# One transformer step: 30 weight pieces are issued from GpSimd's queue in place of SyncE's

## The reference, cut to what matters

```python
mod = silu(cond) @ w_ada + b_ada          # w_ada: 2048 x 12288 f32, for c (latents) and c_ctx (prompt)
sh1, sc1, g1, sh2, sc2, g2 = split(mod, 6)
h = rms_norm(x, norm1_g) * (1 + sc1) + sh1
z = h @ w_in                              # q, k, v of two attentions, and gate logits
o_g, o_d = gqa_attention(...), diff_attention(...)
merged = gate_a * (o_g @ w_branch_a) + gate_b * (o_d @ w_branch_b)
x = x + g1 * (merged @ w_out)
h2 = rms_norm(x, norm2_g) * (1 + sc2) + sh2
x = x + g2 * peer_layer(h2, peer_w_query, ...)   # 128 gathered experts per token
y = rms_norm(x, final_norm_g)
```

## Time and profile before

| | |
|---|---|
| median of 3 runs | 5230.48 us (5229.95 to 5242.82) |
| the profiled execution | 5234.13 us, of it 5232.3 us span |
| TensorE busy in the span | 3333.8 us (64%) |
| VectorE busy | 2689.3 us (51%) |
| GpSimd busy | 1815.6 us (35%) |
| bytes moved | 1885.12 MB, 360 GB/s over the span |
| q0 (GpSimd's DMAs) | 1347.98 MB |
| q1 (SP's DMAs) | 535.33 MB |

### The profile page before, as it was taken

One profiled execution on the slowest core, in us unless ns is written; L12 is line 12 of the kernel. 1 busy time (PEld: TensorE's weight loads), 2 busy tenths in 40 slices (PEclk: granted clock), 3 DMA queues, 4 the chain that ended last, 5 costly groups with the idle time before them and its releaser, 6 DMA issues.

```text
span 5232.3 us, 32559 instructions
## 1 busy us (share of the span) xinstructions
PE 3333.8 (64%) x11312; PEld 1263.2 (24%) x11312; DVE 2689.3 (51%) x3921; ACT 414.4 (8%) x785; POOL 1815.6 (35%) x1365
## 2 busy tenths in 40 slices
PE   4869888898788898899986390001333333333566
PEld 1333343343344443444442240000000000000000
DVE  2320119897133201576758757998655656565200
ACT  0010000000222110111010010000000000000000
POOL 0000003354322000344435334667445454454333
PEclk7979999999799999999998695555555555555566
DMA  9979976898998687898989878889999999999998
GB/s 379 375 272 352 368 256 264 332 367 345 386 365 321 236 294 271 338 379 352 382 343 388 334 316 340 340 350 397 418 421 418 418 418 418 421 418 418 418 415 367
DMA packets 412273, 1885.12 MB, mean 360 GB/s; under 512 B 30544, under 2 KB 34160, under 8 KB 241760
## 3 DMA queue, kind: packets, MB, share of 16 engines
q0 software_dynamic: 187200, 1347.98, 63.5%
q1 hardware_dynamic: 224928, 535.33, 27.6%
HBM read 1845.08 MB, written 39.42 MB: 360 GB/s over the span
## 4 chain that ended last, share of the span: by engine, by line
DMA 43%; PE 36%; DVE 13%; issue 3%; POOL 2%; ACT 1%; SPq 0%; DVEq 0%; POOLq 0%; ACTq 0%; PEldq 0%
PE ps L795 29%; DMA activations<-in_peer_v,zt 27%; DVE big L1859 5%; DMA big<-in_peer_v,zone 4%; DMA big<-in_peer_u,sel 3%; DMA big<-in_w_in 2%; DMA big<-in_w_ada 2%; PE ps L1133 2%; DMA big<-in_peer_v,sel 2%; DVE big L1605 1%; PE ps L895 1%; POOL big L778 1%; DMA big<-in_w_out 1%; PE ps L955 1%; PE ps L846 1%
## 5 line engine op out<-in xcount | busy, mean ns | idle before, releaser
L795 PE MATMUL ps<-big,activations 128*128 128x512 f32 x4096 | 1797.4, 599 | 115.8 <-ACT zt L1144 38.0
L1859 DVE CUSTOM_DVE_ANT_0 big<-big,activations 128x2048 f32<-128x2048 f32 x384 | 867.3, 2290 | 503.2 <-DMA big<-in_peer_u,sel 479.6
L795 PEld LDWEIGHTS ps<-big,activations 128*128 128x128 f32 x4096 | 778.3, 192 | 1122.8 <-issue 1020.2
L778 POOL DMA_INDIRECT big<-in_peer_u,sel x384 | 565.8, 1473 | 581.9 <-DVE zt L1859 497.4
L1133 PE MATMUL ps<-activations 128*32 128x512 f32 x1536 | 352.2, 1009 | 458.1 <-DMA activations<-in_peer_v,zt 458.1
L1133 PE MATMUL ps<-big,activations 128*32 128x512 f32 x1536 | 353.2, 1014 | 431.1 <-DMA big<-in_peer_v,zt 428.3
L1540 DVE CUSTOM_DVE_ANT_0 big<-big 128x2048 f32<-128x2048 f32 x128 | 291.6, 2292 | 146.1 <-DMA big<-in_peer_u,sel 105.6
L1550 DVE SCALAR_TENSOR_TENSOR big<-big,work 128x2048 f32<-128x2048 f32 x128 | 301.0, 2352 | 90.0 <-DMA big<-in_peer_v,sel 87.5
L753 POOL DMA_INDIRECT big<-in_peer_u,sel x128 | 225.9, 1765 | 316.0 <-DVE zone L1605 279.0
L735 POOL DMA_INDIRECT big<-in_peer_v,sel x128 | 235.0, 1836 | 280.9 <-DVE big L1550 219.8
L735 POOL DMA_INDIRECT big<-in_peer_u,sel x128 | 202.5, 1582 | 328.4 <-DVE work L1540 264.4
(11 more groups left out here) (189 smaller groups left out, 2444.5 us busy)
## 6 DMA issues: line engine op xcount, KB each, us to landing
big<-in_w_in SPq DMA_DIRECT2D x84, 2048.0 KB, 9.3
big<-in_w_ada SPq DMA_DIRECT2D x48, 2048.0 KB, 12.4
big<-in_w_out SPq DMA_DIRECT2D x24, 2048.0 KB, 13.0
big<-in_peer_w_query SPq DMA_DIRECT2D x24, 2048.0 KB, 8.8
big<-in_w_branch_a SPq DMA_DIRECT2D x12, 2048.0 KB, 23.3
big<-in_w_branch_b SPq DMA_DIRECT2D x12, 2048.0 KB, 8.8
big<-z_blocks SPq DMA_DIRECT2D x20, 512.0 KB, 14.5
big<-in_peer_u,sel POOLq DMA_INDIRECT x640
```

The source lines that it names most:

```text
L778: pool.indirect_dma_start(u_slot(m), None, eu, bass.IndirectOffsetOnAxis(ap=sel[:, t % 2, k:k + 1], axis=0)).then_inc(u_in[m % UR], 16)
L795: ins = nc.tensor.matmul(bank(bk), acts[:, k, b * P:(b + 1) * P], w[:, n % WS, k], start=(start and k == 0), stop=(stop and k == KT // 2 - 1))
L1859: V.tensor_tensor_reduce(out=x, in0=x, in1=h_of[ph], scale=1.0, scalar=0.0, op0=ALU.mult, op1=ALU.add, accum_out=dots_b[ph % 2][:, st * TO ...
```

## The change

The 30 pieces from 18 on are no longer issued by SP but by GpSimd, in its loop over the panels. Before it waits for panel p, GpSimd issues pieces 4p+1 to 4p+4. Their landings count on three semaphores of their own, `late_in`, one for each slot; what TensorE waits for is recounted (`late_before` gives how many of these pieces went to the slot before). The waits for `w_free`, the order of TensorE's work, the slots and the bytes are the same.

```diff
+LATE = sorted(RING_AT["ada", i] for i in range(ADA_FIRST, 4 * ADA_PR))
+def late_before(n):
+    return sum(m < n and m % WS == n % WS for m in LATE)
...
+        late_in = [sem(f"late_ada_loaded{i}") for i in range(WS)]
...
                 for c in range(QKV_CH):
-                    if p == 0:
-                        ada(A_QKV + c)
                     if c + 1 < QKV_CH:
                         for j in range(2):
                             half(...)
-                    elif p == 0:
-                        ada(A_ATT)
-                        ada(A_ATT + 1)
...
                     keys(0)
                     sp.dma_start(skn..., sub).then_inc(sk_in, 16)
-                    for i in range(2, 5):
-                        ada(A_ATT + i)
...
-                if g == 0:
-                    ada(A_ATT + 5)
...
                     for c in range(DCH):
-                        ada(A_BR + 2 * c)
                         for j in range(2, 6):
                             half(RING_AT["br", 6 * c + j], 0, 0, br(c, j))
-                        ada(A_BR + 2 * c + 1)
...
-                    if g == 0:
-                        ada(A_OUT + c)
...
-                    if g == 0 and c < DCH - 1:
-                        ada(A_QRY + c)
...
+            def ada(i):
+                n = RING_AT["ada", i]
+                pool.wait_ge(w_free, n + 1)
+                pool.dma_start(w_wide[:, n % WS], w_ada[...]).then_inc(late_in[n % WS], 16)
+
             for p in range(ADA_PR):
+                for i in range(4 * p + 1, 4 * p + 5):
+                    if ADA_FIRST <= i < 4 * ADA_PR:
+                        ada(i)
                 pool.wait_ge(ada_sum, p + 1)
                 pool.dma_start(mod[:, p * ADA_W:(p + 1) * ADA_W], ada_st[p % 2]).then_inc(ada_out[p % 2], 16)
                 pool.wait_ge(ada_out[p % 2], 16 * (p // 2 + 1))
                 if p + 2 < ADA_PR:
                     bias(p + 2)
...
             def wait_half(n, i, step):
-                pe.wait_ge(w_in_sem[n % WS], 16 * (n // WS + 1) + i * (16 * step // WS))
+                if n in LATE:
+                    pe.wait_ge(late_in[n % WS], 16 * (late_before(n) + 1))
+                else:
+                    pe.wait_ge(w_in_sem[n % WS], 16 * (n // WS + 1 - late_before(n)) + i * (16 * step // WS))
```

More of the change, by code:

```diff
@@ L713, in _ @@
                                         pattern=[[-1, P]], channel_multiplier=1).then_inc(mats, 1)
+            def ada(i):
+                n = RING_AT["ada", i]
+                pool.wait_ge(w_free, n + 1)
+                pool.dma_start(w_wide[:, n % WS], w_ada[:, (i % 4) * 4:(i % 4) * 4 + 4, (i // 4) * ADA_W:(i // 4 + 1) * ADA_W]).then_inc(late_in[n % WS], 16)
             for p in range(ADA_PR):
+                for i in range(4 * p + 1, 4 * p + 5):
+                    if ADA_FIRST <= i < 4 * ADA_PR:
+                        ada(i)
                 pool.wait_ge(ada_sum, p + 1)
```

## The result

The changed kernel takes 5259.4 us in median of 6 runs (5253.23 to 5263.1), the kernel before 5230.22 (5226.53 to 5242.82). The ratio is 1.0052, with an interval of 1.0038 to 1.0066: 29 us slower. The profiled execution has a span of 5260.7 us, 28.4 above the one before.

What follows compares the result with a forecast made beforehand. TensorE and the DMA engines were taken as both within 5% of full, so arrival order decides. Terms of +8 (qkv), +2.5 (attention), +9 (br) and +9 (out and qry) gave +28.5 us: 5259 in median, range 5228 to 5276.

Steps and rivals of the forecast that it cites:

- The bound and the mechanism: Between 117 and 730 us TensorE and DMA are nearly full; beside a piece on q0 a half gets a third of bytes.
- qkv: Stage of seven chunks from 144.18 to 274.68 us: cycle goes from 18.64 to 19.75 us, +8 us in all.
- Attention: GpSimd issues piece 29 only at about 303.5, behind a store and the bias, but queries come sooner: +2.5, bounds 0 and +5.
- the tight half: Half whose ring predecessors are a piece and a half: wanted in 9.05 us, forecast to land in 12.6, a 3.5 us stall.
- br: Branch stage: at three places (420.33 is the first) the piece is issued with the tight half, 3 us each, +9.
- d: How much later than SP GpSimd could issue the next piece: taken as 1 us; at 2.8 no stall.
- the rival of the late start: If GpSimd's 512-row issue costs like four gathers, the tight half is through before the piece begins: same, 5234; chance 0.27.
- out and qry: Five chunks with the pattern cost up to 3.5 us each, less waits already there: +9, bounds 2 and 14.
- The clock: Stalls may lower TensorE's granted clock in four places, 1.7 to 2.9 us each, adding 7 to 12; only in the range.
- The bytes decide: Rival: DMA engines are full before and after, so one queue more changes nothing: same, 5232; chance 0.14.
- Faster: Rival: pieces start as slots free and halves lose nothing, so some 20 us of TensorE's waits go: 5210; chance 0.05.
- The signs: Halves land in 12 to 13 us, w_in and w_out waits rise 20 or more, w_ada's fall, equal packets, 420-439 step +3.

## Why the prediction was right

**The bound and the mechanism** were right. TensorE and the DMA engines are both nearly full in qkv and br, entries of the ring have 0.7 to 1.4 us of slack, and a second queue breaks the order in which they land. The equal counts of packets that the earlier trace rows show for gathers hold for pieces: 130 to 131. ScalarE's queue gave the same loss, and rows of 2 KB on it, with even bytes, took back 11.3 of the 27.3 us of stages.

By the Trainium skill (DMA: Bandwidth & Descriptors, "Queues, rings and completion order") each DMA engine takes turns between its queues packet by packet. The traces agree in that the counts are equal where both queues are busy: 464 to 465, 130 to 131 and 110 to 106 packets.

**The whole** was forecast as 5259 and measured as 5259.4. This is better than its terms deserve, and luck in good part: two large errors cancel, -7.4 in br and +6.1 in out and qry, the clock was left out of the sum, and what follows the prompt's stages came out only 1.7 us longer, where other kernels had up to 12 less and 10 more.

- *qkv*, +8: it is +6.3, of it 2.9 busy time, nearly all of it the slow half at 232.62. The second half of each chunk, issued just ahead of a piece, landed in 10.1, 11.2, 13.7, 12.8, 10.1, 9.4 and 12.6 us (issued from 161.9 to 278) for the 12.6 that I worked out: three of seven are there, and those of about 10 cost little or nothing.
- *Attention*, +2.5 for a late issue: measured +3.5, but the reason was wrong. Its own pieces cost 0.0; what grew is mostly the tight half of the last chunk (2.7 of the 3.5). The late issue is real and costs 11.5 only where the bytes don't cover it.
- *br*, +9: it is +1.6. The failed step is "GpSimd issues the next piece then, d later than SP could", with d = 1. An issue does take 0.75 us, near the 0.9 of my estimate. But the bytes begin about 4 us behind it, where on idle engines they began 1.2 to 1.5 behind, so d is 2 to 3, and the tight half lands in 9.4 to 9.9 us. There the rival of the late start was right in its effect, not in its cause, an issue as dear as four gathers. It isn't the whole account: with the pieces of br alone the start was as late, and one place still lost 3.7 us. In qkv and out it doesn't help, as the tight half has another half in front of it and is itself late.
- *out and qry*, +9 with 14 as upper bound: it is +15.1, of it 7.3 busy time. One wait, before 646.36, is 6.89 us, where the sum allowed 3.5 at most for a place.
- *The clock* was named and left out of the sum. Busy time is 8.9 us of the 26.5, and some 8 of it are the clock (2.9 in qkv, 7.3 in out and qry, less 2.3 in attention, with split pairs in them).

**The rivals.** *Late start* had 0.27 of chance and came true, in effect, for the pieces of br alone. *The bytes decide* was refuted twice, with the same bytes and 26.5 and 27.3 us more in the prompt's stages: the issuer fixes the queue, and two queues don't keep the order. The Trainium skill (DMA: Bandwidth & Descriptors, "Issuing engines are not separate DMA queues") says that several issuers only save issue time. The runs differ from it by those 26.5 and 27.3 us, and the measurement decides. *Faster*: nothing of it is seen.

**The signs.** Two held: in the overlaps q0 has as many packets as q1, and the latent stages start 26.6 us later (768.13 against 741.50). The others missed. Waits for pieces were to fall and rose from 17.7 to 24.2 us. Waits for w_in and w_out were to rise by 20 us or more and rose by 17.3. The step from 420 to 439 us was to be 3 us longer; it runs from 430.4 to 449.43 now, 19.0 us for 18.9. Only some of the halves took 12 to 13 us.

**What stays open.** Behind the last qry chunk the spans differ by up to 21 us (4509.4 with a quarter of the bytes on GpSimd's queue, 4530.8 with the pieces of br), though no edit touches what runs there, and the whole of the kernel with 2 KB rows on ScalarE's queue grew by 7.8 us where its prompt's stages had grown by 16. The medians of the other kernels followed their stages to within 8 us, so a shift there is paid at the end to about that. What in the gather stages takes or gives back such amounts wasn't tried. Nor was why a queue's first packets come 3 to 4 us behind the issue when another queue is busy. And no kernel issued the pieces from a second queue while keeping the order, or from SP ahead of its stores; that the lost order costs, and not the earlier issue, is argued from the landings.

## What to carry to other kernels

Where a ring of buffers is fed just in time, the queue is part of its schedule: transfers that one queue would land one after another share the engines packet by packet on two, and the one that is wanted first gets the smaller part if its packets are shorter. Before moving an issue to an idle engine, look for entries with less slack than such an overlap costs (here 0.7 to 1.4 us against 1 to 4), and keep these and whatever is issued within some microseconds of them on one queue. And time the stage, not the whole: stages that an edit didn't touch agreed to 2 or 3 us, single runs of the whole only to 10.

## What the runs showed of the hardware that was not expected

- On GpSimd's queue rows of 2 KB and 1 KB still move in packets of about 4 KB (0.52 MB in 126 packets; 0.49 in 136). On the hardware queues of SP and ScalarE a row is a packet (q10 moved the same 44.04 MB in 11088 packets with rows of 4 KB and in 22176 with rows of 2 KB).
- A direct DMA of 512 rows costs GpSimd 0.75 us to issue, little more than the 0.50 for 8 KB.
- Bytes begin about 4 us behind such an issue (432.59 to 436.4 or later), and 3 to 4 us behind one by ScalarE (431.04), while SP's queue is busy. On idle engines they began 1.2 to 1.5 us behind GpSimd's issue (298.17) and within 2 behind SP's (355.24).
- With the pieces of br alone one half was through by 427 us but for some 50 of its 1024 packets, and landed only 4 to 5 us later: beside the piece the last ones came at 13, 4 and 5 in a microsecond.
- Waits of TensorE of 3.7 to 6.9 us were followed by a granted clock of 0.71 to 0.81 over the next half, which then took 8.8 to 10.0 us in place of 7.13. Busy time made a third of the loss.
